# Sixty-four half-sparse tokens instead of thirty-two in a two-block transformer kernel

## The chip, the cores and the metric

The kernel runs on one core of a Trainium2 chip. A core has five engines with queues of their own: TensorE (PE, with its weight loads shown apart as PEld), VectorE (DVE), ScalarE (ACT), GpSimd (POOL) and SyncE (SP), and sixteen DMA engines that all queues share. Work on different engines is ordered by semaphores alone, and each engine takes its instructions in the order in which they were written. The metric is the device time of one execution, in microseconds, as the median of several runs.

## The reference, cut to what matters

Two transformer blocks over 512 tokens of width 1024. Nearly all that the change touches is the last part of the second block, a feed-forward layer that picks 128 of 16384 experts for each token:

```
def block(xb):                                   # xb: (tokens, 1024)
    q = (xb @ w_pq).reshape(PEER_BLOCK, PEER_HEADS, 2, D_KEY // 2)
    s = jnp.einsum("thpd,hpnd->thpn", q, sub_keys)
    s_top, i_top = lax.top_k(s, PEER_TOPK)       # 16 of 128 keys, twice per head
    ...
    best, ci = lax.top_k(cand, PEER_TOPK)        # 16 of 256 pairs for each of 8 heads
    e = i1 * N_KEYS + i2                         # expert number
    gate = jax.nn.softmax(best, axis=-1)
    act = jax.nn.gelu(jnp.einsum("thkd,td->thk", u_exp[e], xb))
    return jnp.einsum("thk,thkd->td", (gate * act), v_exp[e])
```

An expert is a row u (layer one: a dot with the token) and a row v (layer two: what is added to the output, weighted by gate times activation).

## The kernel before

Each fp32 product is made of three products of rounded parts: a weight tile of 128 x 1024 comes by DMA into one of four ring slots, ScalarE rounds it to its high part (line 1411, `split_high`), GpSimd subtracts to get the low part (line 907, `split_low`), and TensorE multiplies high by high, high by low, and low by high (line 2275, `products`).

The expert layers treat the 512 tokens in three ways.

- 128 **sparse** tokens (the first): for each of their 128 picks the row u is gathered by an indirect DMA of GpSimd (line 921, `gather`: 128 rows of 4 KB in one DMA, one pick for each of 128 tokens), and VectorE takes the dot (line 2017, `dot`); later the row v is gathered and added (line 2157, `axpy`).
- `TU` = 352 **dense** tokens: layer one multiplies every one of the 128 tiles of u (128 experts each) with all of them; the activations go to DRAM and come back in layer two, where they are multiplied by the gates (zero for experts not picked).
- `XC` = 32 **half-sparse** tokens (the last): their dots are made with gathered rows, 128 partitions holding 4 picks of each of the 32 tokens, so `CC` = 32 gathers do for all. The gelu of the dots is multiplied into their gates, and layer two takes them with the dense ones (`TD` = 384 columns), with activations of one.

**Layer one**, `for e in range(NE)` with `NE` = 128 tiles: TensorE runs `up(e)`, 24 matmuls of 128 x 128 weights against 352 columns. `w_split` has two buffers, so the parts of tile e+2 are made only when `up(e)` is done. Beside it VectorE searches the picks, with `between(t)` putting dots among the search steps, up to `TOP_DOTS` = 36. From tile `FIRST_SPREAD` = 56 on, 48 batches of eight tokens are **spread**: VectorE makes one-hot matrices of the picks (lines 2140 to 2143) and then one or two dots, TensorE multiplies them out (line 2876, 16 instructions beside each `up`, into three PSUM banks in turn), ScalarE copies the result out of the bank (line 1426) and stores 1 MB for every two batches.

**Layer two**, again 128 tiles: `down(e, c)` makes 18 matmuls of 512 columns. VectorE goes by pairs of tiles: dots or axpys as `dots_by` and `axpys_by` count them, `weigh` of two tiles (activation by gate), their low parts, and the low part of the odd weight tile (`odd_low`, line 2181); GpSimd makes the even ones. Weight parts have four buffers here (`late_split`).

What sets the order around the change is a table of numbers. `gather_after(j)` gives the tile after which GpSimd issues gather j (seven slots, `GR`); `dots_to(n)` runs dots on VectorE up to the n-th. SyncE carries, one behind another: activations out (`hidden`), weight tiles, activations back (`act_back`) and gates. Before layer one TensorE turns x of the sparse tokens into rows in banks 6 and 7 (line 2855, read by the dots), and after `up(2)` x of the half-sparse tokens into banks 2 and 3 (line 2886).

## Time and profile before

| | us |
|---|---|
| median of 3 runs | 2469.8 (2467.21 to 2477.37) |
| the profiled execution | 2464.55, its span 2462.7 |
| PE busy | 2413.0 (98%) |
| DVE busy | 1499.0 (61%) |
| POOL busy | 1279.9 (52%) |
| ACT busy | 953.8 (39%) |

The first tile of layer one starts 1320 us after the span's start, layer two at about 1918 us, and it ends some 20 us before the span does. A busy PE is not a PE at its peak: a matmul lasts longer in the records than the distance to the next one, so the pace has to be read from starts.

### The profile page before, as it was taken

The page shows a single profiled execution, that of the slowest core. Times are in us where ns is not written, and L with a number is a line of the kernel's source. Part 1 is how long each engine was busy: PE and PEld are TensorE (multiplying, and loading weights), DVE is VectorE, ACT ScalarE, POOL GpSimd, SP SyncE. Part 2 cuts the span into 40 slices and gives each one's busy share as a digit, 9 for nine tenths or more (in the row PEclk, how much of TensorE's full clock was granted, in tenths as well). Part 3 has the DMA queues.
Part 4 walks back from the last instruction along what each step waited for, and adds up shares of the span by engine and source line. Part 5 has one row for each costly group of instructions (what it writes and reads, how often), then busy time and mean ns, then how long its engine had stood idle before and what let it go on. Part 6 is the DMA issues. An engine that isn't in the chain of part 4 may idle for free.

```text
span 2462.7 us, 33014 instructions
## 1 busy us (share of the span) xinstructions
PE 2413.0 (98%) x12371; PEld 2031.9 (83%) x12371; DVE 1499.0 (61%) x2649; ACT 953.8 (39%) x1568; POOL 1279.9 (52%) x730
## 2 busy tenths in 40 slices
PE   9999999999999999999999999999999999999998
PEld 6877766878786778788789999999999888888886
DVE  3247255776402825423278698899971688888885
ACT  3256455222223434623333333444433333333333
POOL 3651423444454332144434788666678666565652
PEclk9999999999999999999999999999999999999999
DMA  5320112565433221032222799899999999999992
GB/s 218 120 86 1 61 60 88 203 198 177 154 103 128 72 90 61 26 99 91 101 86 98 262 310 315 294 359 360 358 359 335 345 405 405 403 396 391 397 363 90
DMA packets 217726, 521.57 MB, mean 212 GB/s; under 512 B 19232, under 2 KB 102240, under 8 KB 217184
## 3 DMA queue, kind: packets, MB, share of 16 engines
q1 hardware_dynamic: 124080, 334.09, 38.4%
q0 software_dynamic: 41472, 151.01, 16.5%
q10 hardware_dynamic: 52016, 34.36, 4.4%
q8 instruction: 99, 1.62, 0.3%
q14 instruction: 59, 0.48, 0.1%
HBM read 469.02 MB, written 50.36 MB: 211 GB/s over the span
## 4 chain that ended last, share of the span: by engine, by line
PE 87%; POOL 3%; DVE 3%; ACT 3%; DMA 2%; issue 1%; SPq 0%; ACTq 0%; DVEq 0%
PE bank L2275 59%; PE bank_and L2275 14%; POOL weight_split L891 3%; PE bank L2410 3%; PE bank_and L2876 2%; PE bank_and L2243 2%; DMA ring<-weights 1%; PE bank_and L2400 1%; PE bank L2876 1%; ACT weight_split L1035 1%; DMA arena<-expert_acts 1%; PE bank_and L2375 1%; PE bank L2375 1%; POOL weight_split L907 1%; PE bank L2254 0%
## 5 line engine op out<-in xcount | busy, mean ns | idle before, releaser
L2275 PE MATMUL bank<-h_split,weight_split 128*128 128x352 f32 (+1 forms) x5472 | 1078.9, 355 | 18.1 <-POOL weight_split L891 4.6
L2275 PEld LDWEIGHTS bank<-h_split,weight_split 128*128 128x128 f32 x5472 | 936.7, 188 | 135.1 <-issue 15.5
L891 POOL TENSOR_TENSOR weight_split<-ring,weight_split 128x1024 fp32r<-128x1024 f32 x182 | 453.0, 2489 | 721.9 <-ACT weight_split L1035 721.7
L2275 PE MATMUL bank<-late_weight_split,weighted_split 128*128 128x512 f32 x1512 | 363.8, 389 | 0.0
L907 POOL TENSOR_TENSOR weight_split<-ring,weight_split 128x1024 fp32r<-128x1024 f32 x129 | 310.5, 2408 | 98.7 <-ACT weight_split L1411 98.0
L921 POOL DMA_INDIRECT arena<-weights,arena x288 | 279.4, 970 | 111.8 <-DVE arena L2017 57.6
L2275 PEld LDWEIGHTS bank<-late_weight_split,weighted_split 128*128 128x128 f32 x1512 | 283.7, 188 | 58.8
L1035 ACT ACTIVATE weight_split<-ring 128x1024 fp32r<-128x1024 f32 x182 | 191.9, 1054 | 293.2 <-PE bank L2275 202.3
L1411 ACT ACTIVATE weight_split<-ring 128x1024 fp32r<-128x1024 f32 x130 | 137.5, 1059 | 365.0 <-PE bank L2275 346.3
L907 POOL TENSOR_TENSOR late_weight_split<-ring,late_weight_split 128x1024 fp32r<-128x1024 f32 x63 | 160.3, 2545 | 159.2 <-ACT late_weight_split L1411 159.2
L2017 DVE CUSTOM_DVE_ANT_0 arena<-arena,bank_and 128x1024 f32<-128x1024 f32 x160 | 191.1, 1217 | 62.3 <-DMA arena<-weights,arena 59.6
L2275 PE MATMUL bank_and<-late_weight_split,weighted_split 128*128 128x512 f32 x756 | 192.2, 390 | 1.7 <-DVE weighted_split L2174 1.6
L2157 DVE SCALAR_TENSOR_TENSOR bank_and<-arena,bank_and 128x1024 f32<-128x1024 f32 x127 | 163.6, 1288 | 25.1 <-ACT late_weight_split L1411 16.4
L1444 ACT ACTIVATE weighted_split<-arena 128x384 fp32r<-128x384 f32 x128 | 66.2, 517 | 264.1 <-DVE arena L2168 264.0
L2275 PEld LDWEIGHTS bank_and<-late_weight_split,weighted_split 128*128 128x128 f32 x756 | 141.6, 188 | 32.4 <-issue 3.2
L1411 ACT ACTIVATE late_weight_split<-ring 128x1024 fp32r<-128x1024 f32 x126 | 132.6, 1053 | 58.3 <-PE bank L2275 50.9
L2275 PE MATMUL bank<-hidden_layer_split,weight_split 128*128 128x512 f32 x528 | 122.3, 392 | 1.3 <-POOL weight_split L891 1.0
L2174 DVE TENSOR_TENSOR weighted_split<-arena,weighted_split 128x384 fp32r<-128x384 f32 x128 | 73.1, 571 | 78.7 <-ACT weighted_split L1444 71.5
L2275 PEld LDWEIGHTS bank<-hidden_layer_split,weight_split 128*128 128x128 f32 x528 | 98.3, 188 | 24.9 <-issue 2.6
L2275 PE MATMUL bank_and<-h_split,weight_split 128*128 128x512 f32 x384 | 92.8, 399 | 0.3 <-POOL weight_split L891 0.3
L1584 DVE SCALAR_TENSOR_TENSOR arena<-bank,rstd 128x512 f32<-128x512 f32 x37 | 25.6, 691 | 102.1 <-PE bank L2275 97.0
L2168 DVE TENSOR_TENSOR arena<-arena 128x384 f32<-128x384 f32 x128 | 74.3, 614 | 21.8 <-DMA arena<-expert_acts 17.8
(400 smaller groups left out, 2956.0 us busy)
## 6 DMA issues: line engine op xcount, KB each, us to landing
ring<-weights SPq DMA_DIRECT2D x493, 512.0 KB, 4.7
gates_spread<-arena ACTq DMA_DIRECT2D x24, 1024.0 KB, 12.4
arena<-gates_spread SPq DMA_DIRECT2D x96, 256.0 KB, 7.8
expert_acts<-arena SPq DMA_DIRECT2D x128, 176.0 KB, 4.3
arena<-expert_acts SPq DMA_DIRECT2D x128, 176.0 KB, 8.7
arena<-weights,arena POOLq DMA_INDIRECT x288, 7.4
arena<-bias_sel ACTq DMA_DIRECT2D x1, 2048.0 KB, 7.5
arena<-bias_band ACTq DMA_DIRECT2D x1, 2048.0 KB, 7.9
```

What stands on the lines that cost most here:

```text
L891: nc.gpsimd.tensor_tensor(w_split[:, (count - 1) % 2, 1, :], ring[:, n % RING, :], w_split[:, (count - 1) % 2, 0, :], ALU.subtract).then_i ...
L907: nc.gpsimd.tensor_tensor(w[:, 1, :], ring[:, (BEFORE + e) % RING, :], w[:, 0, :], ALU.subtract).then_inc(w_lo_ready, 1)
L921: nc.gpsimd.indirect_dma_start(gathered_rows[:, j % GR, :], None, expert_rows, bass.IndirectOffsetOnAxis(ap=pick, axis=0)).then_inc(gather ...
L1035: a.activation(w_split[:, s % 2, 0, :], ring[:, n % RING, :], ACT.Copy).then_inc(w_high, 1)
L1411: a.activation(split_of(e)[:, 0, :], ring[:, n % RING, :], ACT.Copy).then_inc(w_hi_ready, 1)
L2017: v.tensor_tensor_reduce(rows_, rows_, x[:, :], 1.0, 0.0, ALU.mult, ALU.add, n).then_inc(gather_used, 1)
L2157: v.scalar_tensor_tensor(out=wide[:, :], in0=rows_, scalar=coef[:, j:j + 1], in1=wide[:, :], op0=ALU.mult, op1=ALU.add).then_inc(gather_us ...
L2168: v.tensor_tensor(by_group(weighed[:, e % 2, :]), by_group(act_in[:, e % AS, :]), gblk[:, b % 2, :, j * GT:(j + 1) * GT], ALU.mult).then_i ...
L2174: v.tensor_tensor(p_split[:, e % PS, 1, :], weighed[:, e % 2, :], p_split[:, e % PS, 0, :], ALU.subtract).then_inc(p_lo_ready, 1)
L2275: ins = mm(*args, start=start, stop=stop)
L2410: last = mm(bank[4 + g % 2][:, h * HD:(h + 1) * HD], probT[:, u % 2, c * P:(c + 1) * P], vals(i, c), start=(c == 0), stop=(c == blocks(i) ...
L2876: mm(bank[2 + n % 3][:, (t % 4) * P:(t % 4 + 1) * P], hot1[:, t % HOT, :], hot2[:, t % HOT, :], start=True, stop=True).then_inc(hot_used, 1)
```

## The change

`XC` goes from 32 to 64. So `TU` is 320, `CC` is 64 gathers, and there are 320 gathers and 192 dots in all where there were 288 and 160. Around it the table of numbers is new:

- the spreading begins at tile 61 instead of 56, and the gathers come about 0.9 to a tile from tile 16 on;
- the dots of the half-sparse tokens run on through batch 18 of the spreading; then banks 6 and 7, which now serve both kinds of dots, are refilled at tile 80; until then the spreading has only banks 2 and 3;
- the half-sparse dots are moved, passed through gelu (ScalarE, tile 83), multiplied into the gates (VectorE, batch 25) and turned (TensorE, tile 88, into bank 4) in the middle of the spreading, not ahead of it;
- in tiles 109 to 127 VectorE makes the low parts of the odd tiles;
- of the dots, 96 are done by the end of the spreading and 120 by the end of layer one (108 and 128 before), 72 are left to layer two (32 before), and the axpys begin at tile 46 instead of 26; both go 10/3 to a pair of tiles instead of 8/3.

The core of the diff:

```
-XC = 32
+XC = 64
...
-        few_x = ctx.enter_context(nc.psum_tensor("bank2_and_3", [P, 2 * T], F32))
...
-        FIRST_SPREAD = 56
-        SPREAD_DOTS = TOP_DOTS + BATCHES * 3 // 2
-        UP_DOTS = SPREAD_DOTS + 20
-        AXPY_FROM = 26
-        FEW_ROWS_AT = 11
-        FEW_DOTS_AT = 47
+        FIRST_SPREAD = 61
+        FEW_LAST = 18
+        FEW_GAP = 3
+        SPREAD_DOTS = 96
+        UP_DOTS = SPREAD_DOTS + 24
+        ODD_FROM = FIRST_SPREAD + BATCHES
+        AXPY_FROM = 46
+        FEW_ROWS_AT = 12
+        FEW_DOTS_AT = FIRST_SPREAD + FEW_LAST + 2
+
+        def dots_in_spread(batch):
+
+            if batch <= FEW_LAST + FEW_GAP:
+                return min(TOP_DOTS + (batch + 1) * 3 // 2, CC)
+            return min(CC + (batch - FEW_LAST - FEW_GAP) * 5 // 4, SPREAD_DOTS)
...
-            return min(UP_DOTS + e // 2 * 8 // 3, UP_ROWS)
+            return min(UP_DOTS + e // 2 * 10 // 3, UP_ROWS)
...
-            return min(max((e - AXPY_FROM) // 2 + 1, 0) * 8 // 3, PICKS)
+            return min(max((e - AXPY_FROM) // 2 + 1, 0) * 10 // 3, PICKS)
...
-            if j < GR:
-                return 15 + j * 2 // 3
             n = j - GR
             if n < TOP_DOTS:
-                return 18 + n
+                return 16 + j * 10 // 9
...
-                    bank[2 + n % 3][:, :].rearrange("p (t k) -> p k t", t=4), ACT.Copy).then_inc(staged, 1)
+                    bank[2 + n % 2][:, :].rearrange("p (t k) -> p k t", t=4), ACT.Copy).then_inc(staged, 1)
...
-                if e in (NE - 4, NE - 3):
-                    weighted_high(e - (NE - 4))
-                if e == FIRST_SPREAD - 4:
+                if e == NE - 2:
+                    weighted_high(0)
+                    weighted_high(1)
+                if e == FEW_DOTS_AT + 2:
                     act_e.wait_ge(few_moved, 64)
...
+                if batch == FEW_LAST + 7:
+                    dve.wait_ge(dots_gelu, 1)
+                    few_gates = chosen[P - XC:P, SEARCH_ORDER[0], 2 * P:3 * P]
+                    v.tensor_tensor(few_gates, few_gates, few_gelu, ALU.mult).then_inc(chosen_ready, 1)
+                elif batch == FEW_LAST + 12:
+                    dve.wait_ge(chosen_turned, ND + 1)
+                    link(v.tensor_copy(gate_row[:, TU:TD], bank[4][:, 0:XC]))
             link(v.memset(act_in[:, :, TU:TD], 1.0))
-            dots_to(UP_DOTS)
+            for e in range(ODD_FROM, NE):
+                if e % 2:
+                    odd_low(e)
+                while dotted[0] < UP_DOTS and gather_after(dotted[0]) <= e - 2:
+                    dot(dotted[0])
+                    dotted[0] += 1
...
-                wait(pe, staged, n - 2)
+                wait(pe, staged, n - 1)
...
+                if e == FIRST_SPREAD + FEW_LAST + 1:
+                    pe.wait_ge(gather_used, CC)
+                    x_to_rows(lambda part, k: h_split[:, part, k, 0:P].bitcast(F32))
```

TensorE at the start of layer one, before (line 2855 turns x of the sparse tokens, 16 products of two instructions each):

```order
L2275 MATMUL bank<-arena 128x128 x3
L2855 MATMUL bank_and<-const,h_split 128x128 x16
L2275 MATMUL bank<-h_split,weight_split 128x352 [waits w_lo_ready]
L2275 MATMUL bank<-h_split,weight_split 128x352 x23
L2275 MATMUL bank<-h_split,weight_split 128x352 [waits w_lo_ready]
L2275 MATMUL bank<-h_split,weight_split 128x352 x23
```

And now:

```order
L2298 MATMUL bank<-arena 128x128 x3
L2298 MATMUL bank<-h_split,weight_split 128x320 [waits w_lo_ready]
L2298 MATMUL bank<-h_split,weight_split 128x320 x23
L2298 MATMUL bank<-h_split,weight_split 128x320 [waits w_lo_ready]
L2298 MATMUL bank<-h_split,weight_split 128x320 x23
```

The 16 products have left this place; they stand behind `up(80)`, with a wait for the 64 half-sparse dots.

GpSimd at the start of layer two, before (line 907 is the low part of an even tile, line 921 a gather):

```order
L907 TENSOR_TENSOR late_weight_split<-ring,late_weight_split 128x1024 [waits w_hi_ready]
L921 DMA arena<-weights,arena 128x1024 [waits gathered_rows_used] x3
L907 TENSOR_TENSOR late_weight_split<-ring,late_weight_split 128x1024 [waits w_hi_ready]
L921 DMA arena<-weights,arena 128x1024 [waits gathered_rows_used] x3
L907 TENSOR_TENSOR late_weight_split<-ring,late_weight_split 128x1024 [waits w_hi_ready]
L921 DMA arena<-weights,arena 128x1024 [waits gathered_rows_used] x2
```

And now (lines 918 and 932):

```order
L918 TENSOR_TENSOR late_weight_split<-ring,late_weight_split 128x1024 [waits w_hi_ready]
L932 DMA arena<-weights,arena 128x1024 [waits gathered_rows_used] x3
L918 TENSOR_TENSOR late_weight_split<-ring,late_weight_split 128x1024 [waits w_hi_ready]
L932 DMA arena<-weights,arena 128x1024 [waits gathered_rows_used] x3
L918 TENSOR_TENSOR late_weight_split<-ring,late_weight_split 128x1024 [waits w_hi_ready]
L932 DMA arena<-weights,arena 128x1024 [waits gathered_rows_used] x4
```

Three pairs of tiles carry ten gathers where they carried eight.

VectorE late in layer two, now (line 2187 an axpy, 2198 `weigh`, 2204 its low parts, 2149 the odd low part); before, the counts of line 2157 were 3, 3 and 2 in turn:

```order
L2187 SCALAR_TENSOR_TENSOR bank_and<-arena,bank_and 128x1024 x4
L2198 TENSOR_TENSOR arena<-arena 128x384 x2
L2204 TENSOR_TENSOR weighted_split<-arena,weighted_split 128x384 x2
L2149 TENSOR_TENSOR late_weight_split<-ring,late_weight_split 128x1024
L2187 SCALAR_TENSOR_TENSOR bank_and<-arena,bank_and 128x1024 x3
```

The counts are now 3, 3 and 4, ahead of each pair's `weigh`.

## Rows read from the trace of the kernel before

**Rows 1.** The page: the span, and the chain that ended last, by engine.

```profile
span 2462.7 us, 33014 instructions
...
PE 87%; POOL 3%; DVE 3%; ACT 3%; DMA 2%; issue 1%; SPq 0%; ACTq 0%; DVEq 0%
```

**Rows 2.** Windows: length, busy of PE, PEld, DVE, ACT, POOL; clock, DMA share, GB/s.

```profile
1420.00:1540.00 120.00, 119.97 (x731) 116.49 (x731) 108.03 (x232) 42.68 (x62) 103.45 (x61) 1.00 0.92 312
1600.00:1830.00 230.00, 230.00 (x1633) 230.00 (x1632) 208.92 (x251) 96.82 (x162) 156.90 (x103) 1.00 1.04 358
...
1940.00:2140.00 200.00, 199.80 (x880) 164.84 (x880) 163.39 (x220) 73.73 (x101) 131.72 (x93) 1.00 1.03 405
2150.00:2390.00 240.00, 240.00 (x1060) 198.76 (x1060) 195.26 (x228) 87.39 (x119) 146.75 (x108) 1.00 1.02 394
```

**Rows 3.** Timeline of PEld: start, length; an up, a spread; one tile of layer two.

```profile
1620.07 3.82 PEld L2275 LDWEIGHTS bank<-h_split,weight_split 128*128 128x128 f32 x24
1623.86 1.91 PEld L2876 LDWEIGHTS bank_and<-arena 128*128 128x128 f32 x16
1625.69 2.38 PEld L2275 LDWEIGHTS bank<-h_split,weight_split 128*128 128x128 f32 x15
...
2104.26 1.32 PEld L2275 LDWEIGHTS bank_and<-late_weight_split,weighted_split 128*128 128x128 f32 x6
...
2108.34 1.32 PEld L2275 LDWEIGHTS bank_and<-late_weight_split,weighted_split 128*128 128x128 f32 x6
```

**Rows 4.** Timeline of layer one ahead of the spreading; the two gelus are 30 tiles apart.

```profile
1423.44 0.45 ACT L1417 ACTIVATE arena<-bank 128x352 f32<-128x352 f32 x1
...
1426.53 1.06 ACT L1411 ACTIVATE weight_split<-ring 128x1024 fp32r<-128x1024 f32 x1 [2.63 <-PE bank L2275]
...
1427.67 2.39 POOL L907 TENSOR_TENSOR weight_split<-ring,weight_split 128x1024 fp32r<-128x1024 f32 x1 [0.54 <-ACT weight_split L1411]
...
1430.17 5.94 PEld L2275 LDWEIGHTS bank<-h_split,weight_split 128*128 128x128 f32 x37 [0.17 <-issue]
...
1541.90 0.45 ACT L1417 ACTIVATE arena<-bank 128x352 f32<-128x352 f32 x1
```

**Rows 5.** A late tile in the timeline of ACT; DMA issues in 1420:1540, us to landing.

```profile
1410.73 1.06 ACT L1411 ACTIVATE weight_split<-ring 128x1024 fp32r<-128x1024 f32 x1 [4.72 <-DMA ring<-weights]
...
ring<-weights SPq DMA_DIRECT2D x31, 512.0 KB, 5.2
```

**Rows 6.** The start of layer one on PEld, and a window after an idle PE.

```profile
1316.15 3.65 PEld L2855 LDWEIGHTS bank_and<-const,h_split 128*128 128x128 f32 x32
...
1320.49 7.71 PEld L2275 LDWEIGHTS bank<-h_split,weight_split 128*128 128x128 f32 x48 [0.69 <-POOL weight_split L907]
...
364.00:366.00 2.00, 1.54 (x4) 1.28 (x5) 2.00 (x3) 0.18 (x1) 0.00 (x0) 0.50 0.00 0
```

**Rows 7.** One batch of the spreading on ACT and DVE.

```profile
1620.38 1.22 DVE L2140 TENSOR_TENSOR arena<-bank,arena 128x1024 f32<-128x1024 f32 x1 [0.96 <-PE bank L2876]
1620.43 0.60 ACT L1426 ACTIVATE arena<-bank 128x512 f32<-128x512 f32 x1
```

**Rows 8.** DMA issues in 1940:2140, median us to landing.

```profile
ring<-weights SPq DMA_DIRECT2D x50, 512.0 KB, 10.2
...
arena<-expert_acts SPq DMA_DIRECT2D x50, 176.0 KB, 10.8
```

**Rows 9.** `weigh` of three pairs in succession on DVE, three and two axpys between.

```profile
2101.66 1.02 DVE L2168 TENSOR_TENSOR arena<-arena 128x384 f32<-128x384 f32 x2
...
2109.82 1.02 DVE L2168 TENSOR_TENSOR arena<-arena 128x384 f32<-128x384 f32 x2
...
2116.59 0.59 DVE L2168 TENSOR_TENSOR arena<-arena 128x384 f32<-128x384 f32 x1
```

**Rows 10.** Waits in 1920:1945, the first six tiles of layer two.

```profile
PEld bank_and L2275 <- issue: 2.8, 3, 1.3
PE bank_and L2275 <- DVE weighted_split L2174: 1.6, 3, 0.9
```

More of the change, by code:

```diff
@@ L415, in build @@
         bank = [ctx.enter_context(nc.psum_tensor(f"bank{n}", [P, T], F32)) for n in range(2)]
-        few_x = ctx.enter_context(nc.psum_tensor("bank2_and_3", [P, 2 * T], F32))
-        bank += [few_x[:, 0:T], few_x[:, T:2 * T]]
-        bank += [ctx.enter_context(nc.psum_tensor(f"bank{n}", [P, T], F32)) for n in range(4, 6)]
+        bank += [ctx.enter_context(nc.psum_tensor(f"bank{n}", [P, T], F32)) for n in range(2, 6)]
         wide = ctx.enter_context(nc.psum_tensor("bank6_and_7", [P, 2 * T], F32))
@@ L2852, in _, with x_to_rows @@
             scores(15)
-            for k in range(KD):
-                for part in range(2):
-                    last = mm(wide[:, k * P:(k + 1) * P], h_split[:, part, k, 0:P].bitcast(F32), ident,
-                              start=(part == 0), stop=(part == 1))
-            last.then_inc(x_rows, 1)
+            def x_to_rows(x):
+                for k in range(KD):
+                    for part in range(2):
+                        last = mm(wide[:, k * P:(k + 1) * P], x(part, k), ident, start=(part == 0), stop=(part == 1))
+                last.then_inc(x_rows, 1)
             def up(e):
                 wait(pe, gelu_ready, e - 1)
-                pe.wait_ge(w_lo_ready, e + 1)
+                pe.wait_ge(*low_made(e))
                 for k in range(KD):
```

55 lines of the change are left out of this document (29 added, 26 removed).

## The prediction, made before the changed kernel was timed

> **What bounds the kernel now.** The chain that ended last is 87% PE over a span of 2462.7 us [rows 1], so the first reading is that each column taken from TensorE is won. That reading has to be checked stage by stage, and the view for it is the one of windows, cut at the stages [rows 2]: it shows PE all but full in each, DVE at 208.92 of 230 us in the spreading, and the DMA engines at a share of 1.03 to 1.04 in the spreading and in layer two. So three limits lie close together, and which of them binds differs by stage. Next comes the pace, from starts in the timeline of PEld [rows 3]. One `up` runs from 1620.07 to 1623.86, 3.79 us for 24 matmuls of 352 columns, 0.158 each; the spread takes the 1.83 us up to 1625.69; a tile of layer two comes every 4.08 us, 18 matmuls of 512 columns, 0.227 each.
>
> Outside the spreading the tile is not 3.79 us: 30 tiles take 118.46 us, 3.95 each [rows 4]. The reason is in the same rows. `up` of one tile is done at 1426.5, ScalarE rounds the tile after next for 1.06, GpSimd subtracts from 1427.67 to 1430.06, and TensorE's next load, which had stood idle for 0.17, begins at 1430.17. With two buffers, two tiles take one `up` plus this loop, so the loop C is 2 x 3.95 - 3.79 = 4.11 us. Half of what is cut from an `up` is given back to the loop there.
>
> **Layer one: the columns.** 32 columns less: between 352 and 512 columns a column costs (0.227 - 0.158) / 160 = 0.00043 us, so a matmul drops by 0.0137 and an `up` by 0.33, to 3.46 us.
> - In the 48 tiles of the spreading TensorE is the bound and the whole 0.33 counts: -15.8 us. VectorE's batch is three products and 1.47 dots up to batch 18, about 1.14 apart: 5.1 us against a new tile of 5.29, where before it idled 0.96 in some batches [rows 7]; it holds, barely. The DMA traffic rises there from 358 GB/s [rows 2] to about 375 (the same tiles and stores in less time), and no row shows this mix faster than 358 for long. Bounds: nothing, or 0.2 us a tile for 19 tiles, 4 us; I take +1.5, as the landings did not grow there and seven slots buffer it.
> - In the 80 tiles outside (61 ahead, 19 behind) the tile becomes (4.11 + 3.46) / 2 = 3.785: 0.165 less, -13.2 us.
> - A weight tile is issued behind the gelu two tiles ahead of its use, so it must land within about two tiles less 2.05 us: 5.85 us now, 5.5 then, against a median of 5.2 [rows 5]. Ahead of the spreading the traffic hardly changes, so a few tiles come late: bounds 0 and 4 us, taken +1.2. Behind it, 24 gathers in 18 tiles, where there was one a tile, raise what a tile moves from 1.23 to 1.39 MB and the rate by a fifth, and landings of 6 us or more cost a quarter of their excess a tile: bounds 0 and 6, taken +2.9.
>
> **Layer one: what is moved.**
> - GpSimd's first gathers came up to two a tile and pushed a weight tile late: ScalarE waited 4.72 us for one, where it waits 2.4 to 2.6 for TensorE anyway [rows 4, 5]. Spread out at 0.9 a tile the excess goes: -2.3 us (bounds 0 and -4).
> - The rows of x for the sparse tokens took 3.65 us right before the first `up` [rows 6], under a wait for the first low part that ended at 1320.49 whatever TensorE did. At tile 80 nothing covers them: +3.7 us. Their wait for the 64 dots costs nothing: VectorE makes batch 18 two tiles ahead.
> - With them gone TensorE stands idle for 4.3 us before the first `up`. After a gap of about 2 us elsewhere the granted clock was 0.50, that is 1.2 GHz [rows 6]. Bounds: nothing, or all 3.5 us of an `up` doubled; I take +1.5. The Trainium skill (TensorE: Matmul & The Clock Gate, Part 1) says the array drops to half rate after an idle stretch; the row agrees. By that rule alone the first `up` would run at half pace, which is the upper bound.
> - Two banks for three: the copy out of the bank ends at 1621.03 [rows 7], the next spread begins at 1623.86 [rows 3]. That 2.8 us, 2.5 with the shorter `up`, covers the tighter wait: 0. The later gelu, the gates' product and the turn lie in ScalarE's, VectorE's and TensorE's slack in the spreading; SyncE's two small transfers hold its queue for one landing, with weight tiles behind them: 0 to 1 us, taken 0. The later search start costs nothing either, since the spreading waits for tile 61 and not for VectorE.
> - VectorE's low parts of ten odd tiles take half of GpSimd's time each, but the even tiles' loop is unchanged, and the pair of tiles is paced by it: 0 (a loss of up to 3 us if a dot waiting for its rows stands ahead of an odd low part).
>
> Layer one: -15.8 + 1.5 - 13.2 + 1.2 + 2.9 - 2.3 + 3.7 + 1.5 = **-20.5 us**.
>
> **Layer two.** TensorE's work is the same, 4.08 us a tile. What a tile needs from DMA: 0.524 MB of weights, 0.180 of activations, 0.197 of gates, 4/3 gathers of 0.524: 1.60 MB, or 392 GB/s, and the window from 2150 has 394 [rows 2]. Ahead of it, 1940 to 2140, the rate is 405 at a share of 1.03 and landings are 10.2 and 10.8 us [rows 2, 8]: there the engines make up a backlog, so I read 405 as the ceiling of this mix. Now a tile needs 0.524 + 0.164 + 0.197 + 5/3 x 0.524 = 1.76 MB: 431 GB/s at 4.08 us, more than 405. The tile stretches to 1.76 / 0.405 = 4.34 us: 0.26 x 116 tiles = +30.2. From this goes what the first tiles lost to the same cause already, 4.4 us [rows 10], and about 3 us of rows and tiles fetched ahead; VectorE adds about 1. **+23.8 us**, bounds +12 and +34.
>
> VectorE alone would bind a little too: pairs take 8.16 us with three axpys and 6.77 with two [rows 9], so about 4.17 + 1.33 an axpy; 39 pairs with 128 axpys make 333 us against 39 x 8.16 = 318. That is +15, less a lead of 2.5, +12 us, and it runs at the same time as the DMA limit, not on top of it. It is the lower bound.
>
> Sum: -20.5 + 23.8 = +3.3 us. The profiled execution took 2464.55 and would take 2468; it lay 5 under the median, so the median goes from 2469.8 to 2473.
>
> **The rivals.**
> - *DMA carries the new load; VectorE sets layer two.* For it: 405 is only what was asked for so far. Against: it is flat over 200 us while landings doubled. -20.5 + 12 = -8.5: 2461. The Trainium skill (DMA: Bandwidth & Descriptors, Specifications) states a fabric ceiling of 435 GB/s, by which 431 would fit and this case would hold; the rows never come near it.
> - *SyncE's queue falls behind (slower).* Weight tiles, activations and gates stand in one queue. An activation may be asked for three tiles ahead, so a tile lasts at least (landing + 1.5) / 3: 4.1 us at the 10.8 of [rows 8], where VectorE's feed to TensorE did stall [rows 10]. It decides from a landing of 11.5 us on; at 11.9 a tile is 4.47, 0.39 x 116 = +45: -20.5 + 45 = +25, 2494.
> - *The loop does not bind* (GpSimd's start overlaps more than I read): 128 x 0.33 = -42 with the same small terms, -35 + 24: 2459 or a little under, 2457 if the late tiles go too.
> - *It doesn't do what it says*: an `up` is paced by weight loads, not columns, since a load is itself long in the records, and 320 columns take as long as 352. Then layer one is +5 at most and the whole +29: 2498. Against: 128 columns go at 0.114 each in the spread [rows 3].
>
> **How the numbers follow.** Half a per cent, 12.3 us, is about what a measurement here can tell from no change. The forecast gets 0.59 (its own range 2461 to 2485), VectorE alone 0.20, SyncE's queue 0.12, the unbound loop 0.06, no shorter `up` 0.03. Under 2457.5 lie a tenth of the forecast, a fifth of the second and half of the loop's: 0.13. Over 2482.1 lie a tenth of the forecast and the two slow cases: 0.21. Same: 0.66. With a tenth left out at each side the range is 2456 to 2489.
>
> **What would show it.** An `up` of 3.46 us; tiles of 3.78 outside the spreading and 5.29 in it; 3.7 us at tile 80; layer two at 405 to 408 GB/s throughout, tiles of about 4.34 us with short waits of TensorE for VectorE's weighted parts, and VectorE waiting for DMA ahead of dots, axpys or `weigh`. Wrong would be: a rate over 415 in layer two, tiles of 4.1 there, or a loop much shorter than 4.11.

## The result, and the profile after

The changed kernel took **2494.6 us** (median of 7 executions, 2484.9 to 2507.1), the kernel before 2467.2 beside it (7 executions, 2463.1 to 2479.3): a ratio of 1.010, 95% interval 1.0076 to 1.0125. It is one per cent slower, and 5.6 us above the upper end of the predicted range. The profiled execution took 2494.4, its span 2492.6.

The executions of most kernels here fall into two groups by their mean granted clock, at 0.992 or more, or under it and some 13 us longer, and six of the first seven executions of the changed kernel lay in the lower group.

The page of the changed kernel, the line that answers to [rows 1]; PE has lost 23 of its 87 points, most of them to DMA and VectorE:

```profile
span 2492.6 us, 33123 instructions
...
PE 64%; DMA 12%; DVE 8%; POOL 6%; ACT 5%; issue 4%; SPq 0%; DVEq 0%; ACTq 0%
```

Windows of the changed kernel, cut as in [rows 2] (length; busy of PE, PEld, DVE, ACT, POOL; clock; DMA share; GB/s). PE is no longer full in layer two, and DMA stands at 401 to 402 GB/s from its first window to its last, where before it moved 405 and then 394:

```profile
1420.00:1540.00 120.00, 116.18 (x763) 111.48 (x761) 111.23 (x268) 44.31 (x64) 104.23 (x62) 1.00 0.91 307
1600.00:1830.00 230.00, 230.00 (x1740) 229.74 (x1739) 212.16 (x242) 102.03 (x173) 151.74 (x96) 1.00 1.01 350
1940.00:2140.00 200.00, 190.15 (x820) 153.67 (x819) 161.75 (x250) 66.37 (x90) 133.28 (x98) 0.99 1.03 401
2150.00:2390.00 240.00, 227.91 (x986) 183.42 (x985) 202.02 (x228) 80.69 (x111) 161.56 (x119) 1.00 1.03 402
```

The same view in the first block's attention, 1100 us ahead of anything that the change touches: first the kernel before, then the changed kernel. The instructions are the same; the granted clock is 0.50, that is 1.2 GHz, and PE gets through 126 of them instead of 232:

```profile
220.00:250.00 30.00, 30.00 (x232) 24.61 (x231) 20.44 (x63) 25.92 (x76) 0.00 (x0) 1.00 0.01 2
```

```profile
220.00:250.00 30.00, 30.00 (x126) 23.72 (x125) 13.45 (x42) 16.89 (x52) 0.00 (x0) 0.50 0.01 1
```

The difference of the two spans, 29.8 us, falls into three pieces, read from the gelus and from the span's end:

| | before | after | difference |
|---|---|---|---|
| first gelu of layer one | 1327.1 | 1344.6 | +17.5, of which 16.3 is the low clock |
| first to last gelu of layer one | 592.2 | 567.4 | -24.8 |
| last gelu to the end | 543.4 | 580.6 | +37.1 |

**Layer one** is as forecast or a little better. Two gelus 30 tiles apart, as in [rows 4], now 113.59 us or 3.786 a tile:

```profile
1410.69 0.42 ACT L1428 ACTIVATE arena<-bank 128x320 f32<-128x320 f32 x1
...
1524.28 0.42 ACT L1428 ACTIVATE arena<-bank 128x320 f32<-128x320 f32 x1
```

PEld around tile 80 (start, length; line 2880 is the exchange of the rows of x, 2901 the spread). The exchange lasts from 1678.38 to 1681.98, 3.6 us with nothing beside it; an `up` and its spread then start 5.30 apart:

```profile
1678.38 3.69 PEld L2880 LDWEIGHTS bank_and<-const,h_split 128*128 128x128 f32 x32
1681.98 1.87 PEld L2901 LDWEIGHTS bank<-arena 128*128 128x128 f32 x16
1683.77 3.52 PEld L2298 LDWEIGHTS bank<-h_split,weight_split 128*128 128x128 f32 x24
...
1689.07 2.06 PEld L2298 LDWEIGHTS bank<-h_split,weight_split 128*128 128x128 f32 x14
```

Behind the spreading the tiles take 4.18 us (71.1 for 17). Waits there, 1840 to 1900 (engine, line, what it waited for; us in total, times, longest):

```profile
ACT weight_split L1422 <- DMA ring<-weights: 25.1, 8, 5.6
POOL weight_split L918 <- ACT weight_split L1422: 21.4, 8, 4.6
DVE weight_split L2149 <- ACT weight_split L1422: 20.6, 6, 4.7
```

**Layer two**: the first and the last odd low part on VectorE, 62 pairs of tiles apart. 539.54 us are 8.70 a pair or 4.351 a tile; before it was 501.58 (from 1927.46 to 2429.04), 8.09 and 4.045:

```profile
1920.33 1.22 DVE L2149 TENSOR_TENSOR late_weight_split<-ring,late_weight_split 128x1024 fp32r<-128x1024 f32 x1
...
2459.87 1.22 DVE L2149 TENSOR_TENSOR late_weight_split<-ring,late_weight_split 128x1024 fp32r<-128x1024 f32 x1
```

DMA issues from 1940 to 2140, as in [rows 8] (count, KB each, median us to landing); the landings have gone from 10.2 and 10.8 us to 12.8 and 13.8:

```profile
ring<-weights SPq DMA_DIRECT2D x46, 512.0 KB, 12.8
...
arena<-expert_acts SPq DMA_DIRECT2D x45, 160.0 KB, 13.8
arena<-weights,arena POOLq DMA_INDIRECT x75, 8.5
```

### The profile page after: what moved, and what is told of

It reads as the page before. It is cut to its first block, busy times and chain, and to the rows that moved or that the text cites. A ratio compares the mean times of both kernels' runs of the same rounds, so it can differ in the third digit from the quotient of the medians.

```text
span 2492.6 us, 33123 instructions
## 1 busy us (share of the span) xinstructions
PE 2406.9 (97%) x12372; PEld 2007.7 (81%) x12372; DVE 1541.3 (62%) x2724; ACT 952.6 (38%) x1568; POOL 1295.8 (52%) x752
## 4 chain that ended last, share of the span: by engine, by line
PE 64%; DMA 12%; DVE 8%; POOL 6%; ACT 5%; issue 4%; SPq 0%; DVEq 0%; ACTq 0%
PE bank L2298 47%; DMA arena<-expert_acts 6%; DMA ring<-weights 5%; PE bank L2901 3%; PE bank L2433 3%; PE bank_and L2298 3%; POOL weight_split L918 3%; POOL weight_split L902 3%; DVE bank_and L2187 2%; PE bank_and L2266 2%; ACT weight_split L1422 1%; PE bank L2423 1%; DVE late_weight_split L2149 1%; DVE arena L2031 1%; ACT weight_split L1046 1%
## 5 line engine op out<-in xcount | busy, mean ns | idle before, releaser
L2298 PE MATMUL bank<-h_split,weight_split 128*128 128x320 f32 (+1 forms) x5568 | 1065.2, 349 | 29.4 <-POOL weight_split L918 12.1
L2298 PEld LDWEIGHTS bank<-h_split,weight_split 128*128 128x128 f32 x5568 | 918.4, 188 | 152.4 <-issue 27.8
L902 POOL TENSOR_TENSOR weight_split<-ring,weight_split 128x1024 fp32r<-128x1024 f32 x182 | 452.8, 2488 | 737.9 <-ACT weight_split L1046 737.7
L2298 PE MATMUL bank<-late_weight_split,weighted_split 128*128 128x512 f32 x2268 | 527.5, 393 | 27.2 <-DVE weighted_split L2204 27.2
L2298 PEld LDWEIGHTS bank<-late_weight_split,weighted_split 128*128 128x128 f32 x2268 | 424.9, 189 | 129.0 <-issue 41.2
L918 POOL TENSOR_TENSOR weight_split<-ring,weight_split 128x1024 fp32r<-128x1024 f32 x119 | 286.7, 2409 | 141.8 <-ACT weight_split L1422 140.6
L932 POOL DMA_INDIRECT arena<-weights,arena x320 | 307.9, 962 | 88.5 <-issue 47.7
L2031 DVE CUSTOM_DVE_ANT_0 arena<-arena,bank_and 128x1024 f32<-128x1024 f32 x192 | 228.0, 1216 | 54.4 <-DMA arena<-weights,arena 47.5
L918 POOL TENSOR_TENSOR late_weight_split<-ring,late_weight_split 128x1024 fp32r<-128x1024 f32 x63 | 171.9, 2729 | 137.2 <-ACT late_weight_split L1422 137.2
L1455 ACT ACTIVATE weighted_split<-arena 128x384 fp32r<-128x384 f32 x128 | 66.3, 519 | 340.5 <-DVE arena L2198 340.4
L2433 PEld LDWEIGHTS bank<-arena 128*128 128x128 f32 x528 | 75.5, 211 | 23.8 <-ACT arena L1081 15.1
L2901 PE MATMUL bank<-arena 128*128 128x128 f32 x768 | 93.5, 275 | 0.0
L2901 PEld LDWEIGHTS bank<-arena 128*128 128x128 f32 x768 | 91.0, 191 | 0.1
```

Of the source, the lines that this page charges most:

```text
L902: nc.gpsimd.tensor_tensor(w_split[:, (count - 1) % 2, 1, :], ring[:, n % RING, :], w_split[:, (count - 1) % 2, 0, :], ALU.subtract).then_i ...
L918: nc.gpsimd.tensor_tensor(w[:, 1, :], ring[:, (BEFORE + e) % RING, :], w[:, 0, :], ALU.subtract).then_inc(w_lo_ready, 1)
L932: nc.gpsimd.indirect_dma_start(gathered_rows[:, j % GR, :], None, expert_rows, bass.IndirectOffsetOnAxis(ap=pick, axis=0)).then_inc(gather ...
L2031: v.tensor_tensor_reduce(rows_, rows_, wide[:, :], 1.0, 0.0, ALU.mult, ALU.add, n).then_inc(gather_used, 1)
L2298: ins = mm(*args, start=start, stop=stop)
L2433: last = mm(bank[4 + g % 2][:, h * HD:(h + 1) * HD], probT[:, u % 2, c * P:(c + 1) * P], vals(i, c), start=(c == 0), stop=(c == blocks(i) ...
```

## The experiments

The theory: DMA's ceiling of some 402 GB/s sets layer two, and the gathers that the change adds there cost 1.3 us each; the rest of the miss is a low clock that has nothing to do with the change. Rivals: VectorE alone sets layer two; SyncE's queue does; the low clock belongs to this program. Four of the kernels (halfaxpy, halfgather, halfboth, cols320) leave a part of the work out, as said at each, and so don't return the reference's numbers; they are there for their time alone. All medians in us, with the executions of a mean clock of 0.992 or more in a column of their own, which is the one to compare:

| kernel | median | before beside it | ratio, 95% interval | clock 0.992 up: median (of so many) |
|---|---|---|---|---|
| again | 2481.7 | 2466.7 | 1.0070, 1.0044 to 1.0097 | 2481.2 (5 of 8) |
| halfaxpy | 2482.1 | 2466.7 | 1.0068, 1.0047 to 1.0088 | 2480.9 (8 of 10) |
| halfgather | 2459.9 | 2466.7 | 0.9977, 0.9956 to 0.9999 | 2458.2 (7 of 10) |
| halfboth | 2458.9 | 2466.7 | 0.9951, 0.9924 to 0.9979 | 2445.4 (4 of 10) |
| actqueue | 2484.1 | 2465.7 | 1.0063, 1.0039 to 1.0087 | 2484.1 (4 of 6) |
| more48 | 2479.7 | 2465.7 | 1.0061, 1.0039 to 1.0083 | 2478.9 (8 of 9) |
| filled | 2480.0 | 2465.7 | 1.0059, 1.0037 to 1.0082 | 2480.0 (7 of 7) |
| cols320 | 2443.8 | 2465.7 | 0.9909, 0.9876 to 0.9943 | 2443.8 (4 of 4) |
| early48 | 2467.8 | 2468.3 | 1.0005, 0.9986 to 1.0025 | 2467.4 (11 of 12) |
| early | 2476.3 | 2468.3 | 1.0038, 1.0013 to 1.0063 | 2475.3 (8 of 10) |
| earlybefore | 2464.5 | 2468.3 | 0.9987, 0.9964 to 1.0009 | 2464.5 (10 of 10) |
| poolodd | 2486.0 | 2468.3 | 1.0085, 1.0052 to 1.0117 | 2485.6 (4 of 5) |
| evened | 2461.6 | 2466.6 | 0.9981, 0.9968 to 0.9995 | 2461.2 (9 of 12) |
| again2 | 2483.0 | 2466.6 | 1.0077, 1.0059 to 1.0095 | 2482.0 (5 of 6) |

The kernel before had 2465.4 to 2467.8 in that last column. So at an equal clock the change costs 15 us, not 27.

### What sets layer two

VectorE given time back, nothing taken from DMA:

```diff
-v.scalar_tensor_tensor(out=wide[:, :], in0=rows_, scalar=coef[:, j:j + 1], in1=wide[:, :],
+v.scalar_tensor_tensor(out=wide[:, 0:T], in0=rows_[:, 0:T], scalar=coef[:, j:j + 1], in1=wide[:, 0:T],
```

> The changed kernel with whole gathers, and the axpys on half of the columns only (half of the output of the sparse tokens is left out), some 0.5 us less each on VectorE, nothing less for DMA. Theory DMA: pairs stay at 8.75 us with 402 GB/s, 2494 or at most 2 us less. Theory VectorE: its cycle of three pairs falls from 25.66 us to TensorE's 24.48, so 8.16 a pair: 40 x 0.59 = 24 us less, 2471.

Measured: 2480.9, as the changed kernel. From the 24th to the 60th odd low part a pair of tiles takes 8.78 us (8.75 there). The window of 2150 to 2390: VectorE has lost 46 of its 202 us of work, and DMA still moves 402:

```profile
2150.00:2390.00 240.00, 226.07 (x976) 181.42 (x975) 155.59 (x227) 83.79 (x108) 162.06 (x118) 1.00 1.03 402
```

DMA given time back, nothing taken from VectorE:

```diff
+half_rows = weights.rearrange("n p (a d) -> (n p a) d", a=2)
...
-nc.gpsimd.indirect_dma_start(gathered_rows[:, j % GR, :], None, expert_rows,
+half = gather_after(j) >= NE
+nc.gpsimd.indirect_dma_start(gathered_rows[:, j % GR, D // 2 if half else 0:], None, half_rows if half else expert_rows,
...
```

The lines left out double the row numbers for these gathers and let VectorE read the half row twice, so that its instructions stay as long.

> The changed kernel, with the gathers that are issued in layer two fetching half rows (256 instead of 512 KB each; VectorE reads the half twice, so its instructions keep their length; the dots and sums of those picks are therefore not the reference's). A tile of layer two then moves 1.32 MB instead of 1.76. Theory DMA (402 GB/s is the ceiling of this mix and sets the pace): the pairs with dots fall from 8.83 us to TensorE's 8.16, the pairs with axpys from 8.75 only to VectorE's own 8.55 (8.09, 8.09 and 9.48 in turn), 14 + 8 us and some 3 at the start of the layer: 25 us less, about 2470 at an equal clock. Theory VectorE (its instructions alone set layer two): no change, 2494. A prediction of the first kind but with VectorE no limit: 37 us less, 2457.

Measured: 2458.2, 23 us under the changed kernel at an equal clock. The gain is near the 25 us forecast; the 2470 isn't met because it was reckoned from 2494, a median of low-clock executions. The same window, and four odd low parts in it: 309 GB/s, and pairs of 8.10, 8.10 and 9.48 us in turn, 8.57 on average, which is VectorE's own pace with ten axpys in three pairs:

```profile
2150.00:2390.00 240.00, 230.66 (x1006) 187.81 (x1005) 206.91 (x234) 79.48 (x112) 172.00 (x122) 1.00 0.87 309
```

```profile
2206.91 1.22 DVE L2159 TENSOR_TENSOR late_weight_split<-ring,late_weight_split 128x1024 fp32r<-128x1024 f32 x1
2215.01 1.22 DVE L2159 TENSOR_TENSOR late_weight_split<-ring,late_weight_split 128x1024 fp32r<-128x1024 f32 x1
2223.11 1.22 DVE L2159 TENSOR_TENSOR late_weight_split<-ring,late_weight_split 128x1024 fp32r<-128x1024 f32 x1
2232.59 1.22 DVE L2159 TENSOR_TENSOR late_weight_split<-ring,late_weight_split 128x1024 fp32r<-128x1024 f32 x1
```

Both together (the two diffs above):

> As the kernel with half gathers, and the axpys work on half of the columns (half of the output of the sparse tokens is left out), some 0.5 us less each on VectorE. Theory DMA, then VectorE: with both taken away TensorE sets the pace, 8.16 us a pair throughout, 37 us less than the changed kernel: about 2457 at an equal clock, 13 less than with half gathers alone. If something third held the layer (the queue of SyncE, GpSimd), the pairs stay above 8.3 us.

Measured: 2445.4 (four executions), 36 us under the changed kernel where 37 were forecast. Pairs of axpys at 8.12 us, PE full again:

```profile
2150.00:2390.00 240.00, 240.00 (x1060) 198.72 (x1060) 167.19 (x244) 87.48 (x119) 170.82 (x123) 1.00 0.92 319
```

So there are three floors for a pair of tiles with axpys, one under another: DMA 8.75, VectorE 8.57, TensorE 8.12 to 8.16. Taking VectorE's work away while DMA binds is worth nothing, and taking DMA's away is worth only the distance to the next floor. That distance is small among the axpys and large among the dots ahead of them: over the first 22 pairs the odd low parts come 8.96 us apart in the changed kernel and 8.09 with half gathers. Some 19 of the 23 us are won there. What makes 402 GB/s the ceiling, the DMA engines or what lies behind them, no run here tells.

SyncE's queue, the slow rival. Its forecast of 2494 is the number that came, so its mechanism needed a test of its own:

```diff
-                if e + AS - 1 < NE:
+                if e + AS - 1 < 6:
                     act_back(e + AS - 1)
...
                 if 0 < e < NE - 1:
                     weighted_high(e + 1)
+                    back = e + 1 + AS
...
+                    if back < NE:
+                        act_e.dma_start(act_in[:, back % AS, 0:TU], acts_dram[back]).then_inc(act_loaded[back % AS], 16)
```

> The changed kernel with the activations of layer two (from the sixth tile on) fetched through ScalarE's queue and not SyncE's, where they stand behind weight tiles and gates. The bytes are the same. Theory DMA: still 402 GB/s, pairs of 8.65 to 8.8 us, 2481 in an execution at a mean clock of 0.993 or more (2494 under 0.992). Theory SyncE's queue: the landings and the waits of `weigh` for activations shrink and the pairs fall towards VectorE's own 8.16 (dots) and 8.55 (axpys): some 22 us less, 2459.

Measured: 2484.1, pairs of 8.78 us, 401 to 402 GB/s. Its DMA issues from 1940 to 2140:

```profile
ring<-weights SPq DMA_DIRECT2D x46, 512.0 KB, 12.3
arena<-gates_spread SPq DMA_DIRECT2D x36, 256.0 KB, 13.0
arena<-expert_acts ACTq DMA_DIRECT2D x45, 160.0 KB, 8.7
arena<-weights,arena POOLq DMA_INDIRECT x75, 10.4
```

The activations land after 8.7 us instead of 13.8, the gathers after 10.4 instead of 8.5, and the pace is the same: the wait has only moved to another transfer. The rival falls. Its own formula shows it too: (13.8 + 1.5) / 3 = 5.1 us a tile, where the tile is 4.35. So the formula is wrong here, and which of its parts is wrong isn't shown.

### What the columns bring

```diff
-x = [h_split[:, part, k, P:P + TU] for part in range(2)]
+x = [h_split[:, part, k, P:P + TU - 32] for part in range(2)]
-last = products(bank[e % 2][:, 0:TU], w, x, k == 0, k == KD - 1)
+last = products(bank[e % 2][:, 0:TU - 32], w, x, k == 0, k == KD - 1)
```

> The kernel before, with `up` multiplying 320 of its 352 columns and everything else as it was (layer one of the last 32 dense tokens is left out). Prediction's theory: an `up` of 3.46 to 3.52 us for 3.79; 80 tiles outside the spreading 0.165 less (13.2 us), 48 inside 0.33 less (15.8 us), together 29 us, 2437 for 2466. Rival, loop not binding: 42 us. Rival, weight loads pace `up`: nothing. Layer two stays at 8.09 us a pair.

Measured: 2443.8, 22 us less than the kernel before, not 29. From the first to the last gelu 572.6 us for 592.2, of which the 44 tiles well inside the spreading give 14.4, 0.327 each as worked out; DMA moved 383 GB/s there and nothing was late. Of the 0.165 forecast for a tile outside, the first 17 tiles give 0.12 and the next 39 give 0.11; at the first and behind the last spread nothing is left of it. The `up` itself is faster; the weight tiles come late for it: from 1340 to 1545 us ScalarE waits 21.0 us for them where it waited 10.7 in the kernel before, and behind the spreading (1810 to 1900, before 1830 to 1919) 23.3 for 8.0. At the first spread, besides, one `up` took 5.06 us, most of it at a granted clock of 0.50, behind an idle stretch of 2.15 us of PEld. PEld, an `up` and its spread in 5.29 us:

```profile
1643.64 3.52 PEld L2275 LDWEIGHTS bank<-h_split,weight_split 128*128 128x128 f32 x24
1647.12 1.90 PEld L2876 LDWEIGHTS bank_and<-arena 128*128 128x128 f32 x16
1648.93 1.18 PEld L2275 LDWEIGHTS bank<-h_split,weight_split 128*128 128x128 f32 x8
```

### Behind the spreading

All low parts of layer one on GpSimd:

```diff
...
-                if e < ODD_FROM or e % 2 == 0:
+                if e < NE or e % 2 == 0:
                     split_low(e)
...
-                if e % 2:
-                    odd_low(e)
```

> The changed kernel with all low parts of layer one on GpSimd, as in the kernel before; only tiles 109 to 127 differ. If VectorE's ten odd low parts are what makes these tiles 4.18 us for the 3.94 forecast, they fall by 3 to 4 us in all. If late weight tiles and 24 gathers in 18 tiles do it (the longest wait of ScalarE for a tile was 5.6 us), they stay at 4.1 to 4.3, or get longer, since GpSimd's issues of gathers then stand in the loop of every tile.

Measured: 2485.6 at an equal clock (four executions), 4 us longer than the changed kernel, with intervals that overlap; the last 17 tiles take 72.9 us for 71.1. VectorE's odd low parts are not what makes these tiles long. Whether they are a small help isn't clear of noise.

SyncE asks for weight tile e+4 ahead of the store of the activations of tile e:

```diff
-                hidden(e)
                 tile(e + RING)
+                hidden(e)
```

> The changed kernel with SyncE asking for weight tile e+4 ahead of the store of tile e's activations in layer one, nothing else. Ahead of the spreading the tiles stay at 3.785 us, the loop of the weight parts; behind it they fall from 4.18 to near 3.8, 6 us less; layer two stays at 8.67 us a pair. 2475 where the changed kernel has 2481. If the tiles behind the spreading were long because of VectorE's low parts, they stay at 4.18.

Measured: 2475.3, 6 to 7 us less. The last 17 tiles take 66.3 us, 3.90 each; 567 us of layer one become 564. At the loop's pace of 3.785 these 17 tiles would take 64.3 us, so 4.8 of the 6.8 us above it came from asking late. The rest stays, and ScalarE still waits for weight tiles there, 18.8 us from 1840 to 1900 for 25.1. The total fell by 6 to 7 us, of which the traces place 3 in layer one and 1 behind it.

The same exchange in the kernel before:

> The kernel before with the same exchange on SyncE. Its tiles outside the spreading are at the loop of 3.95 us and few of them were late (16 tiles to the gathers' start took 4.14 each, 23 more at 4.07): 2 to 5 us less, 2461 to 2464; layer two unchanged at 8.09 a pair.

Measured: 2464.5, 3 us less at an equal clock than the kernel before beside it (2467.8), ratio 0.9987 with an interval that takes in 1.

### The gathers somewhere else

Twelve more dots ahead of the spreading:

```diff
-        TOP_DOTS = 36
+        TOP_DOTS = 48
-        FEW_LAST = 18
+        FEW_LAST = 10
-        SPREAD_DOTS = 96
+        SPREAD_DOTS = 106
-        AXPY_FROM = 46
+        AXPY_FROM = 42
-            return min(UP_DOTS + e // 2 * 10 // 3, UP_ROWS)
+            return min(UP_DOTS + e // 2 * 28 // 9, UP_ROWS)
...
-                return 16 + j * 10 // 9
+                return 16 + j * 5 // 6
```

> The changed kernel with twelve more dots ahead of the spreading (48 for 36), so gathers come 1.2 to a tile from tile 16 on, where DMA moves some 305 GB/s and VectorE stands idle for 11 us; the rows of x are exchanged eight tiles earlier, layer one ends with 130 dots for 120, and layer two has 28/9 dots or axpys to a pair for 10/3. Theory DMA: ten gathers less in layer two are 10 x 0.524 MB / 0.402 = 13 us less there; the tiles ahead of the spreading stay at 3.78 us at some 345 GB/s, or lose up to 3 us by late tiles. So 10 to 13 us less than the changed kernel at an equal clock: 2468 to 2471 where that has 2481, within 5 us of the kernel before. If something else than DMA held layer two, it stays at 2481.

Measured: 2478.9. Layer two did what it should, 524.0 us between the first and the last odd low part for 537.8 in the repeat of the changed kernel, 13.8 us less for ten gathers less. But layer one took 582.5 us, and the forty tiles ahead of the spreading 4.09 each for 3.79. Waits from 1420 to 1540:

```profile
ACT weight_split L1422 <- DMA ring<-weights: 39.5, 13, 4.0
...
PE bank L2298 <- POOL weight_split L918: 11.5, 18, 1.1
```

Two causes stand in these lines: weight tiles that landed after 5.9 us for 5.2, and GpSimd. The next kernel takes the first away: the tables of this one, with SyncE's exchange.

> The kernel with 48 dots ahead of the spreading, and in layer one SyncE asks for weight tile e+4 ahead of the store of tile e's activations, not behind it: the slot is free once the low part of tile e is made, while the store waits for the gelu, a whole `up` later. Expected: ahead of the spreading tiles of 3.79 us again, where 48 dots made them 4.09 (13 of 29 rounds of ScalarE waited for the weight tile, 39.5 us): 12 us less; behind it tiles near 3.8 for 4.2: 6 us less; layer two at 8.45 us a pair as with 48 dots. 2460 to 2463 at a mean clock of 0.993 or more, 3 to 6 under the kernel before. If the tiles were late for want of bandwidth and not for being asked late, nothing changes: 2479.

Measured: 2467.4, the time of the kernel before. The wait for weight tiles is gone, but the forty tiles still take 3.99 each. GpSimd at 1451 shows why: two gathers in one tile, 1.10 and 0.94 us with 0.45 between and ahead, and the low part starts only at 1453.33, so that one tile in five lasts 4.77 us where its neighbours alternate between 3.55 and 4.00:

```profile
1450.98 1.10 POOL L932 DMA_INDIRECT arena<-weights,arena  x1 [0.15 <-issue]
1452.38 0.94 POOL L932 DMA_INDIRECT arena<-weights,arena  x1 [0.30 <-issue]
1453.33 2.40 POOL L918 TENSOR_TENSOR weight_split<-ring,weight_split 128x1024 fp32r<-128x1024 f32 x1
```

So the same ten dots were put where a tile has room for its one gather and a batch for its dot and a half:

```diff
-        TOP_DOTS = 36
+        TOP_DOTS = 40
-        SPREAD_DOTS = 96
+        SPREAD_DOTS = 107
-            return min(CC + (batch - FEW_LAST - FEW_GAP) * 5 // 4, SPREAD_DOTS)
+            return min(CC + (batch - FEW_LAST - FEW_GAP) * 3 // 2, SPREAD_DOTS)
...
-                return 16 + j * 10 // 9
+                return 16 + j
```

(with `FEW_LAST` = 15, `AXPY_FROM` = 42 and the 28/9 of the kernel with 48 dots, and SyncE's exchange.)

> The changed kernel with ten dots taken off layer two and put where their gathers should cost nothing: 40 dots ahead of the spreading (one gather to a tile, for 0.9; never two in one tile, since with 48 dots each second one in a tile held GpSimd's next low part back by 1.2 us), and 3/2 dots to a batch for 5/4 behind the exchange of the rows of x (VectorE 5.1 us of the 5.3 of a batch; DMA moved 312 to 361 GB/s there). SyncE asks for weight tiles ahead of the stores of activations, as in the kernel with the exchange alone. Theory DMA: layer one as there (564 us from first to last gelu, at most 3 more), layer two ten gathers shorter, 13 us: 2462 to 2465 at a mean clock of 0.993 or more, where the exchange alone has 2475 and the kernel before 2467. If a gather costs its 1.3 us wherever it stands, 2475.

Measured: 2461.2 at an equal clock, 14 us less than the exchange alone, and the one kernel here that does all the work and whose interval lies under the kernel before: 0.9981, 0.9968 to 0.9995. A part of that is SyncE's exchange, which the kernel before could have too; beside that kernel (2464.5, from other rounds) it is 3 us ahead. Layer one takes 563.9 us, layer two 523.9 between its odd low parts. The windows of 1760 to 1800, where a dot and a half to a batch raise DMA to 379 GB/s (352 in the changed kernel, 361 with the exchange alone) beside a PE that stays full, and of 2150 to 2390:

```profile
1760.00:1800.00 40.00, 40.00 (x304) 40.00 (x304) 39.10 (x46) 17.38 (x29) 28.56 (x20) 1.00 1.05 379
...
2150.00:2390.00 240.00, 234.56 (x1018) 189.70 (x1018) 200.75 (x230) 84.31 (x115) 161.28 (x116) 1.00 1.03 401
```

### The clock

The changed kernel twice more, and once with two more products where PE stood idle for 0.8 us ahead of the fall:

```diff
-lambda i, c: nsa_v(i, 0, c), begun=4, rest=selected_rest)
+lambda i, c: nsa_v(i, 0, c), begun=4, rest=selected_rest, busy=(2, 0))
```

> The changed kernel once more, unaltered. Two questions. Clock: its profiled execution ran from 218 to 255 us at a granted clock of 0.50, in code that the change does not touch, and was 17.5 us later from there on; six of its seven executions had a mean clock of 0.985 to 0.989 and one 0.995 (2484.9 us). If that is a trait of this program, most executions again have about 0.987 and some 2494 us; if it is luck, some have 0.995 and 2478 to 2485. Layer two: tiles of 4.35 to 4.41 us at 400 to 403 GB/s in either case.

> The changed kernel with two more products of 128 x 512 on TensorE (0.43 us each, results unused) in the first block's attention, at 215 us, just ahead of where the granted clock fell to 0.50 in some executions and not in others (9 of 38 of the kernel before, 8 of 15 of the changed one). Theory: the fall follows from the idle 0.8 us at 216 us, and fillers there end it: no execution has a mean clock under 0.992, median 2481. Rival: it is luck that these fillers don't touch: a quarter to a half of the executions are still at 0.985 to 0.991 and 14 us longer.

> The changed kernel once more, unaltered, for the clock alone: six of its first seven executions had a mean clock under 0.992 and lay at 2494, then three of eight. If that is a trait of the program, at least half of ten more lie there. If it is luck that falls on every kernel alike (13 of 86 executions of the kernel before so far), one to four of ten.

Measured: of the changed kernel 3 of 8 and 1 of 6 executions under 0.992, after 6 of 7 at first; of the kernel before 12 of 97, after 2 of 7 by their times; of the ten kernels made from the changed one 21 of 91, from none of seven to six of ten; of the two made from the kernel before none of 14. (The expectation of the filler gives the first counts wrongly: they were 8 of 38 and 9 of 15.) Layer two is the same in the repeats, 4.34 us a tile at 401 to 402 GB/s. The fall stands in five of the profiled executions, all of the changed kernel or of one made from it, each time at 218 or 219 us, and lasted 6.8 us (both repeats), 20.5 and 27.3 in others, and 37.5 in the first one. In the kernel with evened gathers the mean clock from 220 to 250 us is 0.68:

```profile
220.00:250.00 30.00, 30.00 (x163) 23.59 (x163) 15.83 (x51) 19.85 (x59) 0.00 (x0) 0.68 0.01 2
```

The low group occurs with either kernel, so the change is not needed for it. Whether the changed kernel meets it more often stays open. Without the first seven of each, the changed kernel and those made from it have 25 of 105, the kernel before and those made from it 12 of 111, which would seldom be chance (1 in 80). But the line at 0.992 favours that: the traces of the first kind have another 3 to 7 us at 0.50 at the start of layer one, so their mean stands at 0.994 to 0.996 even without a fall, where the kernel before has 0.997. Counted by time (over 10 us above the median of the executions at 0.992 or more) it is 19 of 105 against 13 of 111, which may well be chance. The cause isn't shown either. TensorE stands idle for 0.78 of the two us from 216 in every kernel looked at but the one with fillers, with a fall behind it (the changed kernel) or without (the kernel before, the changed one with SyncE's exchange). The kernel with fillers had no low execution in seven, but neither had the kernel before with SyncE's exchange in ten.

## Why the prediction was wrong, step by step

**The sum.** Forecast +3.3 us, measured +27 in the comparison and +15 at an equal clock. Twelve of the 24 us missed are the low clock of the first executions; the prediction gave its range nothing for it, though one of the three executions of before that it had lay 8 us above the median. The other twelve are layer two: by the trace it lay 13 us over its forecast and layer one 3 us under, and the medians at an equal clock add some 2. So the step that failed is the sum for layer two: the stretch that it gave to DMA was too short and two of its subtractions too large. The kind of mechanism, a DMA ceiling that lengthens every tile there, was right.

**Layer one, forecast -20.5, measured -23.6** (from the trace: -24.8 between the gelus, +1.2 at its start). Right in nearly each term:
- the `up` fell to 3.52 us on PEld (3.46 forecast) and the tile to 5.30 in the spreading (5.29 forecast) and 3.786 outside (3.785): the loop binds, and half of a gain on TensorE is given back. By the measured `up` the loop is 2 x 3.786 - 3.52 = 4.05 us and not 4.11; the two small errors cancel;
- the exchange at tile 80 cost 3.57 us (gelus 8.87 apart for 5.30; 3.7 forecast); the start cost 1.2 (1.5 forecast). In the kernel with short axpys, at full clock until then, TensorE stood idle for 4.25 us, the clock was 0.52 in the next four, and two `up`s took 9.25 us for 7.06;
- ahead of the spreading hardly a tile was late, 3.78 us each from the 17th gelu to the 59th where the kernel before had 4.02 to its 54th, some 3 us better than forecast; DMA in the spreading cost nothing (381 GB/s from 1640 to 1680; 1.5 was taken);
- **mis-sized:** tiles behind the spreading. 4.18 us for 3.94 forecast, 4 us in 17 tiles more than the term had. The cause was named rightly (late weight tiles), and the kernel that asks for them earlier took 4.8 us out of these 17 tiles.

**Layer two, forecast +23.8, measured +37.1.** TensorE's first and last products of its tiles 2 to 127, in the kernel before:

```profile
1927.01 1.61 PE L2275 MATMUL bank_and<-late_weight_split,weighted_split 128*128 128x512 f32 x6 [0.56 <-DVE weighted_split L2174]
...
2444.24 0.84 PE L2275 MATMUL bank<-late_weight_split,weighted_split 128*128 128x512 f32 x3
```

And in the changed kernel:

```profile
1919.88 4.33 PE L2298 MATMUL bank<-late_weight_split,weighted_split 128*128 128x512 f32 x18 [0.92 <-DVE weighted_split L2204]
...
2472.72 2.21 PE L2298 MATMUL bank<-late_weight_split,weighted_split 128*128 128x512 f32 x9
```

That is 518.1 us and 555.1, and the 37 us between them are the whole of layer two's growth; what lies ahead and behind is equal to 0.1 us. At 4.08 us a tile 126 tiles would take 514.1. Some 2 us at the last two tiles are the same in both kernels. What is left is 2.0 us that the kernel before lost, all in its first tiles, and 39.0 that the changed kernel lost, 0.31 on each of 125. The sum had 4.4 for the first and 30.2 + 1 - 3 = 28.2 for the second. So 2.4 and 10.8 of the 13.3 us are found:

- **a misread row, 2.4 us:** the 4.4 us of [rows 10] add a wait of PEld (2.8) to one of PE (1.6), but the two run side by side. By the starts it was 2.0;
- **a lead without a row, 3 us:** "about 3 us of rows and tiles fetched ahead". Layer one ended at 376 GB/s from 1840 to 1900 and 390 from 1920 to 1940 (346 and 343 before), and layer two was slow from its first tiles, so no lead shows. VectorE's 1 us isn't needed, which takes 1 off;
- **mis-sized, 2.3 us:** 125 tiles ran at the long pace, not 116;
- **mis-sized, 4.8 us:** with the new mix the ceiling was 402 GB/s and not 405. 1.76 MB at 0.402 are 4.38 us a tile; the sum had 4.34 less 4.08. Three GB/s are little, but they are paid 125 times;
- the last 1.7 us lie in the first tiles, where the changed kernel was 4.0 us behind by its sixth tile and the kernel before 1.3. The second and third odd low parts came 10.46 and 9.58 us behind the ones ahead of them, for 9.32 and 8.60.

What the prediction had right is the mechanism: a DMA rate that stays flat at 401 to 402 GB/s through the layer, VectorE waiting for activations and TensorE for weighted parts. The upper bound of +34 was still 3 too low.

**The rivals.** VectorE as the next limit was priced well: with DMA's load taken away the kernel came to 2458.2, 7.7 us under the kernel before, where the rival had 8.5 under it. With both taken away it came to 2445.4, 20.5 under, the forecast of layer one to the tenth, by chance as far as the tenth goes, with four executions. The Trainium skill's fabric ceiling of 435 GB/s (DMA: Bandwidth & Descriptors, Specifications), by which the load would have fitted, was never reached: the highest slice of 5 us in layer two shows 406 in the changed kernel and 413 in the kernel before, and the long windows stop at 402 and 405. SyncE's queue gave the right number for a wrong reason. The unbound loop is refuted by 3.786 us a tile outside the spreading, the `up` paced by weight loads by its 3.52.

## What to carry to other kernels

A change that saves time on the engine that is busiest and pays in bytes has to be priced in both currencies: here a half-sparse token saved 0.74 us of layer one (23.6 / 32), and its one gather cost 1.3 us (0.524 MB at 402 GB/s; ten gathers less were 13.8 us less) in a stage where DMA was full, and next to nothing in a tile or batch that had room for it on DMA, GpSimd and VectorE at once. When a stage comes to a ceiling, multiply the excess by all its tiles, and read a loss already suffered from the starts of the engine that does its work, not from waits of two engines added up. A ceiling that is one per cent lower than read is paid on every tile, and a lead may be subtracted only if a row shows it. A load that stands in a queue behind a store waits for what the store waits for; moving it ahead of the store was worth some 6 us here.

## What the runs showed of the hardware

- Mixed traffic of 512 KB tiles, 160 to 256 KB loads and gathers of 4 KB rows stops at 401 to 405 GB/s with a share of 1.03. Above it, the queues only trade waits: one class of transfers came 5 us sooner, another 2 us later, the sum moved at the same rate.
- TensorE ran at a granted clock of 0.50 for 37.5 us of a stretch of small products in which it was busy all the time, in some executions and not in others of one and the same program; it cost 16 us in the profiled one. In four other profiled executions the fall stood at the same place and lasted 6.8 to 27.3 us. After an idle stretch of 4.25 us at the start of layer one it ran at 0.52 for four.
- A gather mostly occupies GpSimd for 0.93 to 1.10 us (median 0.95, the longest of 320 took 1.7) with up to 0.3 ahead of it. One in a tile was hidden; with two, TensorE waited 1.15 us for the next low part.
